# An encoder layer with an RWKV-7 scan: VectorE's inverse steps and reciprocals in another order within the scan's jobs

## What is computed

```
def step(state, inp):
    r_t, w_t, k_t, v_t, kk_t, a_t = inp
    s_kk = jnp.einsum('bhvk,bhk->bhv', state, kk_t)
    new = (state * w_t[:, :, None, :]
           - s_kk[..., None] * (kk_t * a_t)[:, :, None, :]
           + v_t[..., None] * k_t[:, :, None, :])
    read = state if reverse else new
    return new, jnp.einsum('bhvk,bhk->bhv', read, r_t)
y = outs[0] + outs[1]
mu = jnp.mean(y, -1, keepdims=True)
var = jnp.mean(jnp.square(y - mu), -1, keepdims=True)
y = ((y - mu) * lax.rsqrt(var + GN_EPS)).reshape(B, S, D_RWKV) * lnx_w + lnx_b
```

## Time and profile before

| what | us |
|---|---|
| median of 3 runs | 1957.01 (1947.66 to 1977.97) |
| the profiled execution | 1955.42 |
| its span | 1953.7 |
| TensorE busy in it | 1723.0 (88%) |
| VectorE busy | 1358.9 (70%) |
| ScalarE busy | 811.6 (42%) |
| GpSimd busy | 491.2 (25%) |

### The profile page before, as it was taken

One profiled execution on the slowest core, in us unless ns is written; L12 is line 12 of the kernel. 1 busy time (PEld: TensorE's weight loads), 2 busy tenths in 40 slices (PEclk: granted clock), 3 DMA queues, 4 the chain that ended last, 5 costly groups with the idle time before them and its releaser, 6 DMA issues. The chain is left out here.

```text
span 1953.7 us, 42217 instructions
## 1 busy us (share of the span) xinstructions
PE 1723.0 (88%) x15366; PEld 1267.9 (65%) x15366; DVE 1358.9 (70%) x2513; ACT 811.6 (42%) x1327; POOL 491.2 (25%) x432
## 2 busy tenths in 40 slices
PE   3999999998688889888797699999888999999875
PEld 2787766876577778777645376666666667666532
DVE  4699996663567676765546578877766788888707
ACT  1222223441445455443300155655555566656501
POOL 2000000141644554451113013211111223332114
PEclk9899999999899999999997899999999999999988
DMA  8635853433323313222061389989888899999844
GB/s 274 193 99 173 271 171 99 130 113 98 79 44 63 66 44 72 44 61 60 3 242 54 143 314 339 371 337 345 304 304 301 314 347 345 343 351 346 326 200 199
DMA packets 259760, 389.97 MB, mean 200 GB/s; under 512 B 121923, under 2 KB 195841, under 8 KB 232240
## 3 DMA queue, kind: packets, MB, share of 16 engines
q1 hardware_dynamic: 239392, 354.28, 52.5%
q0 software_dynamic: 19872, 33.60, 4.9%
q10 hardware_dynamic: 367, 0.22, 0.1%
HBM read 368.33 MB, written 58.49 MB: 218 GB/s over the span
## 5 line engine op out<-in xcount | busy, mean ns | idle before, releaser
L2369 DVE TENSOR_TENSOR moe_w_lo<-moe_raw,moe_w_hi 128x1024 fp32r<-128x1024 f32 x272 | 315.1, 1220 | 42.8 <-ACT moe_w_hi L2295 42.6
L2295 ACT ACTIVATE moe_w_hi<-moe_raw 128x1024 fp32r<-128x1024 f32 x272 | 265.4, 1047 | 116.0 <-DMA moe_raw<-in_exp_up 115.6
L2249 PE MATMUL moe_pY<-moe_wd,moe_hT 128*128 128x512 f32 x544 | 248.1, 599 | 0.5 <-ACT moe_hT L2310 0.5
L2239 PE MATMUL moe_pH<-moe_w_hi,moe_x_hi 128*128 128x512 f32 x544 | 219.7, 404 | 12.0 <-issue 7.5
L2173 POOL DMA_INDIRECT moe_xg<-scratch_u2d,moe_idx x70 | 89.1, 1272 | 555.9 <-issue 240.4
L572 PE MATMUL proj_bank<-u_hi,w_hi 128*128 128x512 f32 x536 | 213.7, 399 | 8.4 <-PEq L74 6.8
L2239 PE MATMUL moe_pH<-moe_w_lo,moe_x_hi 128*128 128x512 f32 x544 | 214.3, 394 | 0.0
L2239 PE MATMUL moe_pH<-moe_w_hi,moe_x_lo 128*128 128x512 f32 x544 | 214.1, 394 | 0.0
L572 PE MATMUL proj_bank<-u_hi,w_lo 128*128 128x512 f32 x536 | 210.0, 392 | 0.0
L572 PE MATMUL proj_bank<-u_lo,w_hi 128*128 128x512 f32 x536 | 209.6, 391 | 0.0
L2249 PEld LDWEIGHTS moe_pY<-moe_wd,moe_hT 128*128 128x128 f32 x544 | 100.0, 194 | 100.3 <-issue 99.5
(11 more groups left out here) (414 smaller groups left out, 3139.9 us busy)
## 6 DMA issues: line engine op xcount, KB each, us to landing
moe_raw<-in_exp_gate SPq DMA_DIRECT2D x69, 1024.0 KB
moe_raw<-in_exp_up SPq DMA_DIRECT2D x69, 1024.0 KB
moe_wd<-in_exp_down SPq DMA_DIRECT2D x68, 1024.0 KB
w<-in_w_in SPq DMA_DIRECT2D x59, 512.0 KB, 7.0
pre<-in_ada_w SPq DMA_DIRECT2D x10, 2048.0 KB, 20.5
last_yb<-scratch_ybuf SPq DMA_DIRECT2D x4, 2560.0 KB, 25.5
scratch_rkv<-proj_st SPq DMA_DIRECT2D x24, 256.0 KB, 2.0
last_yb<-scratch_ybuf SPq DMA_DIRECT2D x4, 1536.0 KB, 19.8
```

The source lines that it names most:

```text
L2239: ins = nc.tensor.matmul(pH[:], a[:, k], w[p][:, k].rearrange("p w f -> p (w f)"), start=(k == 0 and n == 0), stop=(k == KC - 1 and n == 2))
L2249: ins = nc.tensor.matmul(pY[h][:], hT[:, f], wd[q][:, f, h * 512:(h + 1) * 512], start=(f == 0), stop=(f == 1))
L2295: nc.scalar.activation(w_hi[p][:, ks].rearrange("p k w f -> p w k f"), raw[p][:, :, ks], ACT.Copy) \
L2369: nc.vector.tensor_tensor(w_lo[p][:, ks].rearrange("p k w f -> p w k f"), raw[p][:, :, ks], w_hi[p][:, ks].rearrange("p k w f -> p w k f") ...
```

## The change

In the arithmetic of stage 0, three instructions: the negation of one off-diagonal element of each block of 2 is a subtraction from `zeros` instead of a TENSOR_SCALAR with -1 (L1644), and in `pairs_of_two` L1611 takes zeros minus A for both columns, so that L1612 only subtracts the product from X. `zeros` is the strip of zeros that was there for clearing DRAM.

In the order of VectorE's odd job: stage 0 of the inverse goes from C5 (behind the U reads of j = 5) to A4 (ahead of them), stage 1 from behind the V reads to ahead of them, stage 3 from ahead of B5 (which holds the two MK reads and the y copy) to behind it. Two quarters of `inverse_deviation` go from A4 behind the RP reads, the other two from ahead of the RP reads to the start of the next even job, behind S0, and part 0 of `merge` follows them there. Behind the last job, what has no next job is done ahead of the last y read. The other engines' programs and SyncE's stay as they are.

```diff
--- before.py
+++ after.py
@@ -1608,8 +1608,8 @@
                     return free_dims(m[:], offset, (step, 4), *dims)
                 two = free_dims(inner, 0, (2, 4), (1, 2))
                 ch.mark(nc.vector.tensor_tensor(two, at(A, 2, (SUB, 2)), at(X, 2 * SUB + 3, (0, 2)), ALU.mult))
-                ch(nc.vector.tensor_scalar(at(X, 2, (SUB, 2)), at(A, 2, (SUB, 2)), -1.0, None, ALU.mult))
-                ch(nc.vector.scalar_tensor_tensor(at(X, 3, (SUB, 2)), at(A, 3, (SUB, 2)), -1.0, two, ALU.mult, ALU.subtract))
+                ch(nc.vector.tensor_tensor(at(X, 2, (SUB, 2), (1, 2)), free_dims(zeros[:], 0, (1, 4), (1, 2), (1, 2)), at(A, 2, (SUB, 2), (1, 2)), ALU.subtract))
+                ch(nc.vector.tensor_tensor(at(X, 3, (SUB, 2)), at(X, 3, (SUB, 2)), two, ALU.subtract))
                 two = free_dims(outer, 0, (2, 4), (1, 2))
                 ch(nc.vector.tensor_tensor(two, at(X, SUB + 2, (1, 2)), at(X, 1, (0, 2)), ALU.mult))
                 ch(nc.vector.tensor_tensor(at(X, 2, (1, 2)), at(X, 2, (1, 2)), two, ALU.add))
@@ -1641,7 +1641,8 @@
                     if p >= 1:
                         v.wait_ge(S["turned_out"], 64 + 64 * p)
                     ch(nc.vector.tensor_copy(A[HD:P], Ain[HD:P].rearrange("q s t -> q t s")))
-                    ch(nc.vector.tensor_scalar(flat_x[:, 1::2 * SUB + 2], flat_a[:, 1::2 * SUB + 2], -1.0, None, ALU.mult))
+                    v.wait_ge(S["zeroed"], 1)
+                    ch(nc.vector.tensor_tensor(flat_x[:, 1::2 * SUB + 2], zeros[:, 0:SUB // 2], flat_a[:, 1::2 * SUB + 2], ALU.subtract))
                     pairs_of_two()
                 elif stage == 1:
                     product(4, 0)
@@ -1709,6 +1710,10 @@
                 Tt, normed, ended, ahead = Tts[d], d == 0 and p + 2 < PAIRS, d == 1 and p >= 1, d == 1 and p + 1 < PAIRS
                 merging = d == 0 and p >= 2
                 fill(J, "S0")
+                if merging:
+                    inverse_deviation(p - 2, 2)
+                    inverse_deviation(p - 2, 3)
+                    merge(p - 2, 0)
                 for j in (4, 5):
                     for h in range(2):
                         o = wait_full(v, ("U", J, h, j))
@@ -1725,7 +1730,7 @@
                         norm_inverse(2)
                         norm_inverse(3)
                     if j == 5 and ahead:
-                        invert(p + 1, 0)
+                        invert(p + 1, 1)
                     for h in range(2):
                         o = wait_full(v, ("V", J, h, j))
                         o = o[:, 0:NU * C].rearrange("p (u t) -> p u t", u=NU)
@@ -1741,10 +1746,10 @@
                     if j == 4 and merging:
                         merge(p - 2, 2)
                     if j == 5 and ahead:
-                        invert(p + 1, 1)
                         invert(p + 1, 2)
+                    fill(J, f"B{j}")
+                    if j == 5 and ahead:
                         invert(p + 1, 3)
-                    fill(J, f"B{j}")
                     if j == 4:
                         if normed:
                             norm_floor(p + 2)
@@ -1752,13 +1757,9 @@
                             norm_inverse(1)
                         if merging:
                             merge(p - 2, 3)
-                        if ended:
-                            inverse_deviation(p - 1, 0)
-                            inverse_deviation(p - 1, 1)
+                        if ahead:
+                            invert(p + 1, 0)
                         fill(J, "A4")
-                if ended:
-                    inverse_deviation(p - 1, 2)
-                    inverse_deviation(p - 1, 3)
                 for k in range(4):
                     o = wait_full(v, ("PR", J, k))
                     cs = pair_of(J, k)
@@ -1767,9 +1768,12 @@
                     ch.wait()
                     now_read(nc.vector.tensor_tensor(RP[:, cs, 1], rep(eye[:], 2), o[:, :, 1], ALU.subtract), ("PR", J, k))
                 if ended:
-                    merge(p - 1, 0)
+                    inverse_deviation(p - 1, 0)
+                    inverse_deviation(p - 1, 1)
                 fill(J, "E")
-            for n in range(1, 4):
+            inverse_deviation(PAIRS - 2, 2)
+            inverse_deviation(PAIRS - 2, 3)
+            for n in range(4):
                 merge(PAIRS - 2, n)
             output(JOBS - 1)
             centre(("MEAN", PAIRS - 1, 0))
```

## The result

| what | before | after |
|---|---|---|
| median of 4 runs | 1967.49 us (1947.66 to 2000.0) | 2008.02 us (1992.33 to 2039.68) |
| the profiled execution | 1955.42 | 1992.33 |
| its span | 1953.7 | 1990.6 |

The ratio of the times is 1.0211, with a 95% interval of 1.0128 to 1.0295: the change makes the kernel slower, by 1.3 to 3.0%. The forecast was 1960 us (1942 to 1978), so it had the sign and missed the size by a factor of eight: +36.9 us between the two profiled executions, where +4.7 was summed.

The account below looks back on a forecast made before the run. It took TensorE as the scan's bound on average, busy 403.56 of 460 us. Terms -3.6 + 0 + 2 + 2.8 + 2.3 + 1.2 = +4.7 us on 1955.4 gave 1960 us, range 1942 to 1978.

Parts of the forecast that it names:

- part 1: MK reads before the last inverse stage: TensorE gains up to 28.9 us, 4.1 a job, then waits for Tn instead.
- the sign of being right: TensorE's waits: MK falls from 28.9 to under 5 us, Tn rises from 28.2 to 45 to 55 us.
- Part 2: Inverse's end in odd jobs: copy to XT 1.2 us earlier in jobs 7, 9 and 11, -3.6 us in all.
- Part 3: U reads behind stage 0 end 2.4 us later; the delay counted as hidden, 0 us.
- rival B: Late U reads not hidden, 2.4 us in each of seven jobs: +19.5 us, 1975 us; chance 0.15.
- Parts 4 and 5: Late grams in jobs 1 and 3, +2 us together; job 13's MK reads ahead of stage 3, +2.8 us (2.0 to 3.6).
- Part 6: Half clock behind longer Tn waits, at the head of even jobs: 0.57 us in four more passages, +2.3 us.
- Part 7: Moved reciprocals: 0 within the jobs, +1.2 us at the end of the scan, ahead of the merge.
- Part 8: Stage 0's new arithmetic over the strip of zeros on VectorE: counted as 0.
- The way through DRAM: From the inverse's end at 731.06 to 742.45 in job 7, SyncE's DMAs out and back: 11.39 us, not shortened.
- A: Rival: the expected gain comes, inverse 2.1 us earlier in six jobs: -8.6 us, 1947 us; chance 0.22.
- C: Rival: inverse ends where it did, TensorE's wait moves whole from MK to Tn: 0 to +1 us, 1956 us; chance 0.23.

Follow-up runs that it names:

- e9: Changed kernel with stage 3 back ahead of the MK reads and the old stage 0 arithmetic; 1973.83 us in one run, timed again 1983.98 us, ratio 1.0052.
- e2: Changed kernel with stage 0 back behind the U reads of j = 5, stage 1 following it there; 1978.75 us, ratio 1.0165.
- e3: Kernel before with stage 3 moved behind the MK reads as the only edit; 1987.53 us, ratio 1.0233.
- e4: Changed kernel with five extra, unused TensorE products ahead of its wait for Tn in even jobs; 1993.95 us, ratio 1.0315.
- e7: Kernel before with stage 3 alone behind the MK reads, plus five extra TensorE products in the wait for Tn; 1973.32 us in one run.
- e12: Changed kernel with the old arithmetic of stage 0, only the order being the change's; 1983.0 us in one run.
- the fillers: The two runs e4 and e7, with five extra products in TensorE's wait for Tn; 1993.95 us and 1973.32 us.
- e6: Kernel before with only the deviation's reciprocals and the first part of the merge moved as in the change; 1950.23 us beside 1947.35.
- e5: Kernel before profiled a second time, unchanged; 1949.72 us beside 1947.35 on the same chip.

## Why the prediction was wrong

The frame held. The MK reads gave what part 1 says (the MK waits are gone, TensorE is 4.1 us sooner before the Tn wait in job 7, as forecast), and all of it went into the Tn wait (62.5 us in all, where 45 to 55 was named as the sign of being right), because the path runs from the scan instruction over XT and DRAM to the next even job. What was wrong is how much later that path would get. Point by point:

- **Part 2, the inverse's end: -3.6 us forecast for jobs 7, 9 and 11, +1.0 measured.** The step that failed is "Then the MK read, the y copy and the MK read, some 2 us, from 725.4 to 727.4", which let VectorE find the first MK product done. In job 7 the second stage was over at 742.11, 11.6 us behind the scan instruction (forecast 11.0), but VectorE waited 1.05 us for the first MK product, because that product was 2.2 us later than before. Stage 3 had depended on VectorE alone; now it depends on TensorE's fills, these on V, these on the U reads, these on stage 0 and this on GpSimd and a DMA; and at half clock TensorE takes longer over all of it. Of the 2.2 us, 1.5 were that half clock (e9's job 7 has 0.6 without it). I had added up VectorE's own queue and had not followed that chain. Stage 1, for which I took 2.2 us (half of 4.4; the mean of 4.4 and 1.6 would have been 3.0 and the inverse 0.8 us later), took 1.5 us (736.81 to 738.36), less than either end: it fell into a gap of GpSimd's (2.08 us there, 1.85 in the trace of before). The collisions went into stage 0, with 4.3 us (732.08 to 736.37) where 3.4 were taken.
- **Part 3, the U reads: 0 forecast.** They end at +6.3 instead of the +5.0 forecast, and the weights of the second MK product come 2.2 us later (+13.24 against +11.07). The cover of 2.5 us, read off GpSimd's L1207, nearly held as long as the clock stayed up: in job 7 of e9 the product was 0.6 us late. It did not hold at half clock, which the forecast had only behind Tn. The 9 us of e2 are the whole early place of stage 0, its wait for the grams (part 4) included. The effect is rival B's in kind, but e9, with U reads as late, has its XT sooner than before: they can harm it only because stage 3 had been hung behind the MK reads.
- **Parts 4 and 5, jobs 1, 3 and 13: +4.8 forecast, +8.6 measured,** with +1.6 and +1.8 in jobs 1 and 3 where +2 was set for both, and +5.2 in job 13, where the range ended at 3.6. In job 13 the forecast was better than that looks. The five other kernels with stage 3 behind the MK reads (e2, e3, e4, e7, e12) have +2.9 to +3.1 there, as forecast. The first MK read of job 13 in after and in e12:

```profile
931.20 0.69 DVE L1597 TENSOR_TENSOR rwkv_MK<-rwkv_bank,mg 128x512 f32<-128x512 f32 x1 [2.87 <-PE rwkv_bank L1259]
...
926.66 0.69 DVE L1597 TENSOR_TENSOR rwkv_MK<-rwkv_bank,mg 128x512 f32<-128x512 f32 x1 [0.97 <-PE rwkv_bank L1259]
```

The wait, 0.97 us in e12, was taken as 0 to 1.6. In after it was 1.9 us longer, and in the 5 us before it the granted clock was 0.66, where it was 1.00 in the same stretch of e12:

```profile
925.00:930.00 5.00, 4.17 (x88) 4.10 (x88) 3.13 (x7) 1.18 (x4) 0.00 (x0) 0.66 0.02 3
```

Job 5, counted with 0, has +4.0: its grams were late too, 2.88 us. The DMA wait of the copy of A in job 7 came as forecast in kind, 1.53 us where 1.1 was taken.
- **Part 6, the clock: 0.57 us for each of four passages forecast, 2.7 us measured in three** (6.84, 6.84 and 6.86 us from Tn to the T reads in the jobs behind 5, 7 and 9), and 1.3 to 1.5 us behind jobs 1, 3 and 11. Six passages paid it, not four. The step that failed is the subtraction 4.67 - 4.10: the first is the head of job 14 at half clock, the second the head of job 8 at full clock, and job 8's head has the norm's product over rwkv_sq in it, which job 14's has not. A head of like work is that of job 12, in the kernel before:

```profile
864.36 1.01 PEld L1259 LDWEIGHTS rwkv_bank<-rwkv_Tn,rwkv_RB 64*64 64x64 f32 x32 [0.68 <-DMA rwkv_Tn<-scratch_turned]
```

with its T reads on VectorE:

```profile
867.26 0.82 DVE L1733 TENSOR_TENSOR rwkv_Tt<-rwkv_Tt,rwkv_bank 128x256 f32<-128x256 f32 x2 [0.48 <-PE rwkv_bank L1259]
```

2.90 us at full clock, so that the price stood there as 4.67 - 2.90 = 1.77 us. The product over rwkv_sq comes on top in the others. In job 8 before:

```profile
744.69 0.30 PEld L1259 LDWEIGHTS rwkv_bank<-rwkv_sq,sum 128*128 128x128 f32 x2
745.75 1.01 PEld L1259 LDWEIGHTS rwkv_bank<-rwkv_Tt,rwkv_U 64*64 64x64 f32 x32 [0.76 <-issue]
```

and after:

```profile
763.59 0.50 PEld L1259 LDWEIGHTS rwkv_bank<-rwkv_sq,sum 128*128 128x128 f32 x2
...
765.59 1.01 PEld L1259 LDWEIGHTS rwkv_bank<-rwkv_Tt,rwkv_U 64*64 64x64 f32 x32 [1.50 <-issue]
```

2.00 instead of 1.06 us, and 1.77 + 0.94 = 2.71 us is what was measured. (In the 4.67 us the clock was back for the last product of the head, as it was in job 8 after; where it stayed down, to job 12 in e2 and e3, that head took 5.08 us, 2.18 more than 2.90.) The loads of Tn alone, 1.01 against 1.78 us for the same 32, say the same. It was +12.8 in sum instead of +2.3, and the fillers show 9 to 13 us of it to be real.
- **Part 7, the reciprocals:** nothing in the jobs, as forecast (e6). The last y read came 6.18 us behind the RP reads instead of 5.17, +1.0 where +1.2 stood. The tail as a whole grew by 2.8 (2.0 in e6), because what follows was slower too: the next y read came 2.77 us behind it instead of 1.98 and the reciprocals' wait for ScalarE was 3.60 instead of 2.66 us, with a granted clock of 0.67 in 992 to 1009 us where it was 0.90 in the 15 us before the end in the kernel before:

```profile
992.00:1009.00 17.00, 7.47 (x99) 4.01 (x96) 11.06 (x16) 2.57 (x6) 0.00 (x0) 0.67 0.00 1
```

- **Part 8, the zeros:** worth nothing, as forecast; in job 7 after and e12 have the same times instruction by instruction. Of the eight L1645 the median was 1135 ns (L1644's was 1130), and L1611 took up to 1250 ns with two SBUF inputs in after and up to 1247 ns as TENSOR_SCALAR in e12. The Trainium skill, "SBUF — State Buffer", section "Who interferes with whom", says that a VectorE instruction with two SBUF inputs contends with a GpSimd instruction that reads SBUF, and that TENSOR_SCALAR can contend in its 2-port modes; the trace agrees. Reading L1610's undisturbed 167 ns as a property of the form would have been wrong: it follows the instruction that has just waited.
- **The way through DRAM** was set at 11.39 and left alone. It was 12.00, 11.91 and 11.70 us in jobs 7, 9 and 11 (11.39, 10.80 and 11.47 before), +3.5 over all. DMA issues with their median time to landing, before, 728 to 745 us:

```profile
scratch_turned<-rwkv_X SPq DMA_DIRECT2D x2, 64.0 KB, 2.8
```

and after, 745 to 762 us:

```profile
scratch_turned<-rwkv_X SPq DMA_DIRECT2D x2, 64.0 KB, 3.8
```

The last of the four issues took 1.69 us on SyncE's queue instead of 0.68. Why it did wasn't tried. Since e3 shows +2.0 and e5, the kernel before itself, +1.4, part of it may be chance.
- **The rivals.** A fell, since no gain reached the scan's end; C had the right account of TensorE's wait moving from MK to Tn, but takes XT to stand still; B had the sign and a cause that is a part of the loss. None had the cause that weighs most: that the move of stage 3 alone puts XT behind two products and two reads (e3: +26.5 to +30.8 us), by itself and with nothing else changed. I had priced the 2 us of reads that stand ahead of stage 3 and set them off against reads gained elsewhere, instead of asking what the move costs with the rest left as it was. From the rows of before that would have been: MK reads and y copy ahead, +2 us on XT in each of seven jobs, 14 us (+12.0 measured), and the Tn wait with it over 3 us in each and half clock behind it.
- **The range** ended at 1978 us, because B was cut off there. It should have held B and the clock together. By their terms B with the clock piece as measured is 19.5 - 2.3 + 12.8 = +30 us.

## What to carry to other kernels

Where an engine waits twice in a row, find which of the waits belongs to the chain that sets the end, and price a move by what it puts in front of that chain's last step. Taking away the other wait here only lengthened this one, and a wait of 6 us instead of 1 cost 2.7 us more behind it through the clock. An instruction that depended on its own engine alone and is moved behind a read of another engine's product takes over that engine's whole chain; follow it back to the start before writing "hidden".

Between runs of a few per cent spread, the length of the stage that the change touches, read from first to last instruction in the trace and taken twice for the same kernel, tells more than the whole time.

## What the runs showed of the hardware

- The granted clock was 0.50 in the 6.8 us around the load of Tn after TensorE had waited 6.14 us for Tn, and 1.00 after it had waited 1.11. The same head of the even job took 6.83 and 4.10 us. The mean clock was also 0.53 over 3.5 us of job 7 (738.0 to 741.5) behind a wait of 2.74 us, and 1.00 in the same place of e9 behind one of 2.68. In e7, with five useless products put into the wait and 1.23 us of idling left, it took 4.10 again. The Trainium skill, "TensorE: Matmul & The Clock Gate", section "HAM oscillation — how this bites in real kernels", describes it for waits on a DMA in a loop: the clock falls in the wait and the products behind it start at the lower rate. The trace agrees in kind: in all seven passages of after the T reads came later behind Tn than before, and in six of them later than with the filler; the seventh was the one where 5.00 us of waiting were left with it.
- A VectorE instruction of 8 or 16 columns took 0.17 us or 1.1 to 1.3 us, and each of the long ones ran beside a GpSimd operation on 512 columns; of the six in a row in stage 0 two or three waited in jobs 7, 9 and 11, in both forms of the arithmetic, and the copy of 256 columns in front of them too. In job 13, where GpSimd is silent, all six took 0.17 us.
- The experts' stage, the same in all kernels here, took between 758 and 805 us from profile to profile, and the scan of one kernel 4 to 7 us more or less. What makes the difference no run here shows.
